# Two more seven-product pairs in the second feed-forward product

## What is computed

```python
h = rms_norm(x, norm_ffn[l])
gate_up = jnp.einsum('btd,df->btf', h, w_ffn_in[l])
ff_gate, ff_up = jnp.split(gate_up, 2, axis=-1)
x = x + jnp.einsum('btf,fd->btd', jax.nn.silu(ff_gate) * ff_up, w_ffn_out[l])
```

## Time and profile before

| | us |
|---|---|
| median of 3 runs | 2150.42 |
| lowest, highest | 2149.86, 2151.22 |
| the profiled execution's own time | 2150.78 |
| its span in the trace | 2149.2 |
| PE busy | 2138.8 (100%) |
| DVE busy | 1726.5 (80%) |
| ACT busy | 1262.1 (59%) |
| first double step of FFN_OUT | 1204.80 to 1322.82 |
| second double step | 1322.82 to 1441.4 |

### The profile page before, as it was taken

One profiled execution on the slowest core, in us unless ns is written; L12 is line 12 of the kernel. 1 busy time (PEld: TensorE's weight loads), 2 busy tenths in 40 slices (PEclk: granted clock), 3 DMA queues, 4 the chain that ended last, 5 costly groups with the idle time before them and its releaser, 6 DMA issues.

```text
span 2149.2 us, 30395 instructions
## 1 busy us (share of the span) xinstructions
PE 2138.8 (100%) x10188; PEld 1793.5 (83%) x10188; DVE 1726.5 (80%) x2098; ACT 1262.1 (59%) x1490; POOL 138.2 (6%) x218
## 2 busy tenths in 40 slices
PE   9999999999999999999999999999999999999998
PEld 9988888888888888888888888888888888888886
DVE  5578788666565698999899887787889999998776
ACT  5365455456544665555555556557667666666655
POOL 2021433201000000000000000000000000000000
PEclk9999999999999999999999999999999999999999
DMA  7666555575555566666656666666666666656664
GB/s 242 188 189 215 157 153 149 174 239 176 181 185 185 182 206 200 197 197 200 203 189 196 199 193 199 193 205 184 207 206 186 193 192 196 191 180 212 194 191 153
DMA packets 211515, 412.37 MB, mean 192 GB/s; under 512 B 13176, under 2 KB 13280, under 8 KB 211296
## 3 DMA queue, kind: packets, MB, share of 16 engines
q1 hardware_dynamic: 208608, 402.70, 60.8%
q0 software_dynamic: 1920, 5.31, 0.8%
q10 hardware_dynamic: 896, 3.15, 0.5%
HBM read 409.01 MB, written 3.16 MB: 192 GB/s over the span
## 4 chain that ended last, share of the span: by engine, by line
PE 99%; DVE 0%; DMA 0%; ACT 0%; issue 0%; DVEq 0%; SPq 0%; ACTq 0%
PE gp L1959 48%; PE gp L1891 37%; PE mx L1959 10%; PE mx L2197 1%; PE mx L2081 1%; PE mx L2246 1%; DMA x_tok<-x_in 0%; PE mx L1939 0%; PE mx L2084 0%; PE mx L2078 0%; PE mx L2133 0%; PE mx L2177 0%; PE mx L2092 0%; PE mx L2121 0%; PE mx L2182 0%; PE mx L1923 0%
## 5 line engine op out<-in xcount | busy, mean ns | idle before, releaser
L612 ACT ACTIVATE w_hi<-raw 128x1024 fp32r<-128x1024 f32 x759 | 797.1, 1056 | 666.7 <-PE gp L1891 249.2
L1182 DVE TENSOR_TENSOR w_lo<-raw,w_hi 128x1024 fp32r<-128x1024 f32 x759 | 921.9, 1230 | 235.5 <-ACT w_hi L612 226.9
L1959 PE MATMUL gp<-w_hi,a_hi 128*128 128x512 f32 x1060 | 416.2, 393 | 0.0
L1959 PE MATMUL gp<-w_lo,a_hi 128*128 128x512 f32 x1060 | 413.0, 390 | 0.0
L1959 PE MATMUL gp<-w_hi,a_lo 128*128 128x512 f32 x1060 | 412.8, 389 | 0.0
L1959 PEld LDWEIGHTS gp<-w_hi,a_hi 128*128 128x128 f32 x1060 | 199.1, 188 | 43.0 <-issue 2.7
L1959 PEld LDWEIGHTS gp<-w_lo,a_hi 128*128 128x128 f32 x1060 | 199.0, 188 | 41.6
L1959 PEld LDWEIGHTS gp<-w_hi,a_lo 128*128 128x128 f32 x1060 | 199.2, 188 | 39.9
L1891 PE MATMUL gp<-w_hi,a_hi 128*128 128x512 f32 x576 | 230.0, 399 | 0.0
L1891 PE MATMUL gp<-w_lo,a_hi 128*128 128x512 f32 x576 | 224.8, 390 | 0.0
L1891 PE MATMUL gp<-w_hi,a_lo 128*128 128x512 f32 x576 | 224.4, 390 | 0.0
(11 more groups left out here) (414 smaller groups left out, 3358.0 us busy)
## 6 DMA issues: line engine op xcount, KB each, us to landing
raw<-a_w_in_in SPq DMA_DIRECT2D x192, 512.0 KB, 4.4
raw<-w_ffn_in_in SPq DMA_DIRECT2D x176, 512.0 KB, 4.5
raw<-w_in_in SPq DMA_DIRECT2D x175, 512.0 KB, 3.9
raw<-w_ffn_out_in SPq DMA_DIRECT2D x88, 512.0 KB, 4.6
raw<-a_w_out_in SPq DMA_DIRECT2D x64, 512.0 KB, 4.7
raw<-w_out_in SPq DMA_DIRECT2D x32, 512.0 KB, 4.3
raw<-w_proj_a_in SPq DMA_DIRECT2D x16, 512.0 KB, 4.4
raw<-w_proj_b_in SPq DMA_DIRECT2D x16, 512.0 KB, 4.6
```

Of the source, the lines that this page charges most:

```text
L612: act.activation(w_hi[:, slot], raw[:, slot], ACT.Copy).then_inc(hi_ready, 1)
L1182: dve.tensor_tensor(w_lo[:, slot], raw[:, slot], w_hi[:, slot], ALU.subtract).then_inc(lo_ready, 1)
L1959: ins = pe.matmul(out_, stat[sp_], mov[mp], start=start and p == 0, stop=stop and p == 2, skip_group_check=True)
```

## The change

Pair 20 of the first double step and pair 6 of the second become seven-product pairs; both were plain.

```diff
 MIXED_FIRST = (4, 6)
 MIXED_LAST = (2, 4)
-MIXED_OUT = ((4, 8, 12, 16), (10, 14, 18))
+MIXED_OUT = ((4, 8, 12, 16, 20), (6, 10, 14, 18))
 MIXED_V = (6,)
```

## The result

| | before | the change |
|---|---|---|
| median of 16 runs, us | 2150.15 | 2154.38 |
| lowest to highest | 2149.25 to 2151.22 | 2153.48 to 2158.37 |
| ratio to before (95% interval) | | 1.0021 (1.0015 to 1.0028) |
| the profiled execution, us | 2150.78 | 2154.48 |
| its span | 2149.2 | 2152.9 |

The change saves six matmuls and makes the kernel 4.2 us slower. That lies on the line of 0.2% which the prediction had drawn (4.3 us): 0.197% by the two medians, 0.21% by the ratio in the table. The interval leaves out 1, so the change is slower; whether it passes the 0.2% it doesn't tell. A second set of 11 runs gave 2155.38 against 2150.14 for 33 runs of before beside it (1.0022, 1.0013 to 1.0031).

A forecast was written before the change was run, and what follows sets the result against it. TensorE, busy throughout, was taken as the bound: -1.36 saved, +3.9 seam, +1.66 pair 6, +0.2 restarts, +0.35 later pairs give +4.75 us, so median 2155.2 (forecast itself 2154.4 to 2156.6); range 2153.3 to 2157.2.

The forecast's parts named there:

- The bound and the saving: TensorE is busy the whole span, so six matmuls fewer at 0.2267 us save 1.36 us.
- The seam, first wait: Start of the second double step: TensorE waits 1.86 us plus the load's lateness for the first L1455.
- L: How late the raw unit for pair 20's sums lands: 0 to 1.0 us, taken as 0.7.
- The seam, second wait: Second unit of the second double step: TensorE waits 1.36 us for the second L1455.
- The clock rival (d): Clock falls to 1.2 GHz behind a wait, 2.72 us more per unit: +7.5 to +13 us, chance 0.03.
- Pair 6: Second double step: TensorE waits 1.66 us for sf_lo, whose sums can't start before s_lo.
- Pairs 10, 14 and 18: Second double step: rounds of VectorE and loads take 20.4 to 21.6 us against TensorE's 21.08; 0.35 us in all, bounds 0 to 1.4.
- place 3: Pairs 10, 14 and 18 of the second double step: 0.35 us in all, bounds 0 and 1.4.
- the restarts: Two restarts of TensorE after waits at 0.1 us each, 0.2 us in the sum.
- rival (a): Loads land early, lateness near 0 at pair 20, later pairs even out: +3.5 to +4.3 us, chance 0.33.
- Rival (b): Waits are covered at the seam, only the six matmuls remain: -1.36 us, 2149.1, chance 0.06.
- Rival (c): Loads become the bound at pairs 10, 14, 18 and 20, each round 0.5 us and more: +6 to +8 us, chance 0.05.

The follow-up runs named there:

- early order: Kernel before with FFN_OUT's four activation sums two steps sooner and sf_hi, sf_lo ahead of the second unit's split and t_lo: 0.0 us against before, ratio 1.0000.
- pair 20 alone: Kernel before with only pair 20 of the first double step made a seven-product pair, second double step unaltered: +3.3 us against before, ratio 1.0015.
- The new order: The change with the four L1443 behind the releases of both banks at the seam and the second L1455 one step sooner: +1.2 us against before, ratio 1.0006.
- the run with early sums: The change, same lists, with activation sums two steps sooner and sf_hi, sf_lo ahead of the second unit's split and t_lo: +2.0 us against before, ratio 1.0008.
- The filled run: The change plus ten 128x128 matmuls of ones in the gap where TensorE waits at the seam: +5.3 us against before, ratio 1.0022.

## Why the prediction was right, and where not

**The bound and the saving**: right. TensorE's spacing is unchanged, six instructions are gone, and once all waits are away the stretch is 1.35 us shorter than that of before in the same early order.

**The seam, first wait**: right in its mechanism and near in size. The parts of pair 20 came 13.47 us after its sums, to the hundredth, and L1455 at once behind L1443. L was 0.43 us in the trace where I took 0.7 (sums at 1302.07, 7.95 us ahead of the pair in place of 8.38), which by my own terms gives 2.29 and not 2.56. It was 2.20, since TensorE started 0.05 us behind the L1455 and not 0.14; in the second trace 2.30, with pair 20 alone 2.31. The new order shows the cause: the four L1443 moved, and the wait went.

**The seam, second wait**: this step failed. I had 1.36 us of wait at full clock; there was none, and 1.71 us of slow matmuls stood there. Two of my own signs, a wait at the second unit and clock 1.00, were not met. The clock rival (d) was right that the clock would fall, which I gave 0.03, and wrong in its price: I added 2.72 us and more for each slow unit to the sum, as if nothing else were late at that time. The row on which I leaned, clock 1.00 in the first 10 us, holds two gaps of 1.3 and 0.7 us, the first of them ahead of TensorE's first matmul, and neither as long as this one; it bore on shorter gaps than the one that I had worked out myself. The rule of the Trainium skill that I had set against it ("TensorE: Matmul & The Clock Gate", "Why this matters for your kernels": idle gaps between bursts can drop TensorE to its lower clock) agrees with the trace behind the gap of 2.2 us; behind 1.65 us at pair 6 and behind 1.73 and 1.22 us in the run with early sums the granted clock stayed 1.00. The filled run shows why the sum came out near all the same: when the clock stays up, the second wait is there instead. That the seam as a whole took 2.20 + 1.71 = 3.91 us where I had 3.9 is luck: the slow unit cost 0.35 more than the wait that I had put there, and the first wait was 0.36 less.

**Pair 6**: right, 1.64 to 1.65 us measured against 1.66, in all five traces that have pair 6 in the old order.

**Pairs 10, 14 and 18**: the size was off, 0.03 and 0.08 us in the two traces of the change against 0.35, but inside the bounds; the 1.9 us of the filled run are above my upper end of 1.4. What I called a loop of VectorE and loads is there, but it isn't steady. In the first trace the load for pair 10 took 5.2 us, less than either of the two that I had read (5.4 and 6.6), the sums of pair 10 came 20.5 us after those of pair 6, and the room was back at 0.67 us; with 7.1 us for that load pair 10 waited 0.91.

**The sum**: +4.75 predicted, +4.2 measured in the first set, +5.2 in the second. In the first trace the 0.6 us between are place 3 (0.03 for 0.35) and the restarts (0.1 at pair 6, and one of 0.1 fewer at pair 16, for 0.2). The median, 2154.38, lies at the very foot of the forecast (2154.4 to 2156.6) and inside rival (a)'s numbers (2154.0 to 2154.7); that of the second set, 2155.38, is in the forecast alone. Of (a)'s mechanism the first trace has the half: place 3 cost nothing, but L was 0.43 and not near 0. Rival (b) fell: nothing covered the waits. Rival (c) did not happen in the traces of the change; the filled run comes near to it.

## What to carry to other kernels

Where one engine is busy all the time, a change that takes work from it and gives work to another is to be judged by that other engine's row at the places where the first waits for it: the row's length and the moment at which it can start, not its mean load (80% here). Before adding work there, put what releases the busy engine first and what nobody waits for behind it, and move what needs no late input into idle time; the same change that cost 4 us then left no wait in the trace. If the saving is 0.06% of the kernel, one such place eats it.

## What the hardware showed that I had not expected

- Behind an idle gap of 2.2 to 2.3 us TensorE fell to 1.2 GHz in three of three traces (granted clock of 1320 to 1328: 0.79 in the first trace of the change, 0.81 in the second, 0.79 with pair 20 alone), in two of them at its first matmul, in the other at its fourth, for eight or nine matmuls. Filled with ten small matmuls, it did not (1.00). Behind 1.65 us at pair 6 it stayed at 2.4 GHz in all five traces. Whether the length alone makes the difference no run tells.
- The slow clock cost little here (about 0.4 us of 1.71, by 4.48 us from release to second unit against 4.12 with the gap filled), because the next release came only then. A slow stretch is a cost only as far as it outlasts what is late anyway.
- One and the same load of 512 KB, the last of four issued within 4 us, landed 5.2 and 6.3 us after its issue in two executions of the same kernel, and 7.1 us in the kernel with the filled gap.
